# Late constants behind the fifth unit, decay and delta-rule products spread between units, three units chunk by chunk

## The chip, the cores and the metric

The kernel runs on one core of a Trainium2 chip. The metric is the device time of one execution in microseconds (us), as the median of several executions. TensorE (PE) multiplies, VectorE (DVE) and ScalarE (ACT) do the elementwise work, SyncE (SP) issues nearly all DMAs, and GpSimd (POOL) does nothing that matters here.

## The reference, cut to what matters

Two transformer blocks run on 256 tokens of width 1024. The first has three mixing branches (softmax attention with a decay, `ya`; a gated delta rule, `yb`; stick-breaking attention, `yc`), each gated and projected, then attention over 256 memory tokens and a feed-forward part with a convolution. The second has a retention/convolution mixer and a mixture of 64 experts. What the change touches is the delta rule of the first block, over chunks of 64 tokens:

```python
def step(state, xs):
    q_n, u_n, w_n, g_n, attn_n, kt_n, gl_n = xs
    v_new = u_n - jnp.einsum("bhck,bhkv->bhcv", w_n, state)
    o = (jnp.einsum("bhck,bhkv->bhcv", q_n * jnp.exp(g_n)[..., None], state)
         + jnp.einsum("bhce,bhev->bhcv", attn_n, v_new))
    state = state * jnp.exp(gl_n)[..., None, None] + jnp.einsum("bhck,bhcv->bhkv", kt_n, v_new)
    return state, o
```

There are four chunks and four heads. `decay` in the reference is the matrix exp(gc_i - gc_j) within a chunk, from the running sum `gc` of the gate's logarithm.

## The kernel before

**Units.** The dense weights come as 101 units of 1 MB (128 partitions x 2048 numbers), in the order of the list `UNITS`. SP loads each into one of `RAW` = 5 places of a ring. ACT rounds it to a high part (`ahead`, L1001, `w_high`, 3 places) and DVE takes the difference as the low part (`lows`, L1555, `w_low`, in the unit's own place). PE multiplies in three products for each 128x128 block: high by high, low by high, high by low (`product`, L323 to L325). A unit is 48 such matmuls with 256 columns. `unit` runs all eight input chunks for the first half of the outputs, then for the second; with `by_chunk=True` it runs both halves for a chunk before it goes to the next, so that it asks for a late chunk later. Before a chunk whose input may not be ready it waits (`chunk_ready`). `unit_tok` is the same with tokens as output rows, `unit_o` the one for four-chunk inputs.

**Order.** Each engine's order is written out by hand. In the program of SP (end of the listing), the first five units, x, and the constants are issued with no wait, and unit n waits for the end of unit n-5. `c1` holds constants; its first 744 columns are needed early, the other 4096 (2 MB), `rows_w` (272 KB) and `router_b` (36 KB) are the late ones. They stand ahead of unit 3 (`gk1`).

**Beginning.** PE multiplies `gq0`, the mean square of x, `gq1`, then `gk0`, which needs the normalised input: DVE scales chunks (L1522, `a_h`), ACT rounds them (L984, `h_high`), DVE takes the low part (L1519, `h_low`). On ACT the high part of unit 3 stands ahead of these roundings (`ahead(UNITS[0], 3)`, then `high_parts`). DVE then takes low parts of units and does the convolution taps of each unit (L1600).

**Decay.** After the units `fk0`, `fk1`, PE makes small products with four input rows: L433 (the per-token columns) and L440 (`decay0`, `decay1`: four matmuls of 256 columns that spread a row over all partitions). ACT takes their exponentials (L1087), DVE subtracts (L1658), and then `fv0`, `fv1` follow on PE.

**Delta rule.** `state_v(n)` (L564) multiplies the state; DVE makes `vnew(n)` of it; `state_o(n)` makes the output of chunk n: for each head one matmul with the state (L576, all 128 rows of the array, 64 columns) and one with `vnew` (L578, 64 rows, 64 columns), and then in the same function the state's increment (L586, `dS`, 64 rows, 128 columns), which DVE's `state(n)` adds (L1784, L1786). These steps, and the scores (`sb_scores`, L503) and sums (`sb_sums`, L513) of stick-breaking attention, stand between the units of the branches in the lists that `branch` is given.
**End.** After the dense units the experts run one after another; each expert's weights are 6 MB, and SP loads them as places come free.

## Time and profile before

| | |
|---|---|
| median of 3 runs | 1659.66 us (1658.47 to 1661.39) |
| span of the profiled execution | 1659.8 us |
| PE busy | 1357.1 us, 82% of the span |
| DVE busy | 643.6 us, 39% |
| ACT busy | 489.9 us, 30% |
| read from HBM | 515.81 MB, 311 GB/s over the span |

No separate time stands beside the profiled execution's span, and the span is within 0.2 us of the median. Times in the rows count from the span's start. PE's busy time counts a pipelined matmul as long as it takes from its start to its end, so that successive ones overlap: how long one really costs is the distance between starts. The granted clock (PEclk) is 1.00 at 2.4 GHz and 0.50 at 1.2 GHz.

### The profile page before, as it was taken

How to read it: one execution, taken by the hardware profiler on the slowest of the kernel's cores; microseconds unless marked ns; L12 is line 12 of the kernel's file. 1: busy time of each engine (PE TensorE's matmuls, PEld its weight loads, DVE VectorE, ACT ScalarE, POOL GpSimd, SP SyncE). 2: the span in 40 equal slices, each digit the busy share in tenths (PEclk: the TensorE clock that was granted, in tenths of full speed). 3: DMA queues.
4: the chain of work that ended last, by engine and by line, in shares of the span. 5: the costliest groups of instructions: out<-in, count | busy, mean ns of one | idle time of the engine just before them, and what ended most of it. 6: DMA issues, size and time to landing. Idle time of an engine off the chain costs nothing.

```text
span 1659.8 us, 32820 instructions
## 1 busy us (share of the span) xinstructions
PE 1357.1 (82%) x14402; PEld 1079.8 (65%) x14402; DVE 643.6 (39%) x1008; ACT 489.9 (30%) x819; POOL 0.2 (0%) x4
## 2 busy tenths in 40 slices
PE   8999999999999999998875766765585676567666
PEld 8998899999999999996543433433343343344333
DVE  6787735878787778663110100101110010111001
ACT  5766466456554455432000000000000000000001
POOL 0000000000000000000000000000000000000000
PEclk9999999999999999999998988988898898899889
DMA  7442023453446665488999999999999999999997
GB/s 300 160 146 102 27 102 104 176 195 136 177 180 243 229 246 193 150 350 362 428 425 432 426 429 434 429 428 428 430 429 430 431 429 425 432 430 429 428 431 321
DMA packets 41401, 517.93 MB, mean 312 GB/s; under 512 B 4720, under 2 KB 4848, under 8 KB 6384
## 3 DMA queue, kind: packets, MB, share of 16 engines
q1 hardware_dynamic: 41184, 516.71, 75.9%
q8 instruction: 55, 0.90, 0.2%
q10 hardware_dynamic: 144, 0.17, 0.0%
q14 instruction: 18, 0.15, 0.0%
HBM read 515.81 MB, written 1.05 MB: 311 GB/s over the span
## 4 chain that ended last, share of the span: by engine, by line
PE 47%; DMA 42%; DVE 6%; ACT 3%; issue 1%; SPq 1%; another core or an unknown queue 0%; DVEq 0%; ACTq 0%; PEldq 0%
DMA e_gu<-experts 41%; PE psum L323 10%; PE psum L324 9%; PE psum L325 9%; PE psum L887 6%; PE psum L928 3%; DVE w_low L1555 1%; DMA w_raw<-dense 1%; PE psum L541 1%; PE psum L383 1%; ACT w_high L1001 1%; PE psum L934 1%; PE psum L525 1%; PE psum L392 0%; PE psum L898 0%
## 5 line engine op out<-in xcount | busy, mean ns | idle before, releaser
L887 PE MATMUL psum<-e_gu,x_xt 128*32 128x256 f32 x3072 | 220.0, 450 | 172.7 <-DMA e_gu<-experts 172.7
L887 PEld LDWEIGHTS psum<-e_gu,x_xt 128*32 128x32 f32 x3072 | 109.4, 129 | 276.2 <-DMA e_gu<-experts 184.8
L323 PE MATMUL psum<-h_high,w_high 128*128 128x256 f32 x896 | 256.9, 287 | 4.6 <-DVE h_low L1519 3.6
L324 PE MATMUL psum<-h_low,w_high 128*128 128x256 f32 x896 | 253.7, 283 | 0.0
L325 PE MATMUL psum<-h_high,w_low 128*128 128x256 f32 x896 | 253.5, 283 | 0.0
L1555 DVE TENSOR_TENSOR w_low<-w_raw,w_high 128x2048 fp32r<-128x2048 f32 x100 | 228.5, 2288 | 38.0 <-ACT w_high L1001 33.0
L1001 ACT ACTIVATE w_high<-w_raw 128x2048 fp32r<-128x2048 f32 x100 | 191.2, 1914 | 71.4 <-PE psum L325 54.4
L2206 DVE COPY x_yb<-psum 128x256 f32<-128x256 f32 x64 | 27.2, 425 | 419.7 <-PE psum L928 419.7
L323 PEld LDWEIGHTS psum<-h_high,w_high 128*128 128x128 f32 x896 | 170.9, 191 | 6.1 <-issue 3.8
L324 PEld LDWEIGHTS psum<-h_low,w_high 128*128 128x128 f32 x896 | 171.2, 191 | 0.4 <-issue 0.2
L325 PEld LDWEIGHTS psum<-h_high,w_low 128*128 128x128 f32 x896 | 170.9, 191 | 0.0
L2204 DVE TENSOR_TENSOR x_act<-x_sil,psum 128x128 f32<-128x128 f32 x64 | 18.2, 285 | 335.7 <-ACT x_sil L1473 335.7
L928 PE MATMUL psum<-e_dn,x_actT 128*32 128x256 f32 x2048 | 126.7, 383 | 26.6 <-ACT x_actT L1477 25.3
L1473 ACT ACTIVATE x_sil<-psum 128x128 f32<-128x128 f32 x64 | 17.9, 279 | 431.6 <-PE psum L887 431.6
L928 PEld LDWEIGHTS psum<-e_dn,x_actT 128*32 128x32 f32 x2048 | 59.6, 109 | 75.2 <-issue 25.3
L1475 ACT ACTIVATE x_scat<-psum 128x256 f32<-128x256 f32 x64 | 24.6, 384 | 282.8 <-PE psum L914 280.8
L934 PE MATMUL psum<-x_yb,x_scat 32*128 32x256 f32 x1024 | 73.3, 400 | 34.8 <-DVE x_yb L2206 34.8
L934 PEld LDWEIGHTS psum<-x_yb,x_scat 32*128 32x128 f32 x1024 | 46.2, 184 | 67.1 <-DVE x_yb L2206 65.7
L898 PEld LDWEIGHTS psum<-x_s,x_htok 128*128 128x128 f32 x512 | 58.4, 192 | 5.7 <-issue 5.7
L898 PE MATMUL psum<-x_s,x_htok 128*128 128x128 f32 x512 | 61.4, 278 | 0.6 <-DVE x_s L2150 0.6
L1509 DVE RECIPROCAL all_sq<-all_sq 128x256 f32<-128x256 f32 (+1 forms) x25 | 50.1, 2004 | 12.8 <-ACTq L973 12.5
L323 PE MATMUL psum<-act_high,w_high 128*128 128x256 f32 x176 | 49.7, 282 | 1.2 <-DVE w_low L1555 1.1
(447 smaller groups left out, 2162.0 us busy)
## 6 DMA issues: line engine op xcount, KB each, us to landing
e_gu<-experts SPq DMA_DIRECT2D x44, 4096.0 KB, 52.9
w_raw<-dense SPq DMA_DIRECT2D x100, 1024.0 KB, 4.8
e_dn<-experts SPq DMA_DIRECT2D x46, 2048.0 KB, 49.4
e_dn<-experts SPq DMA_DIRECT2D x36, 1024.0 KB, 54.8
e_gu_lo<-experts SPq DMA_DIRECT2D x16, 2048.0 KB, 51.5
e_gu_hi<-experts SPq DMA_DIRECT2D x16, 2048.0 KB, 55.9
e_gu<-experts SPq DMA_DIRECT2D x8, 1024.0 KB, 8.1
e_gu<-experts SPq DMA_DIRECT2D x2, 2560.0 KB, 10.3
```

What stands on the lines that cost most here:

```text
L323: mm(ps, w[0], src[0], start=start, stop=False, **kw)
L324: mm(ps, w[0], src[1], start=False, stop=False, **kw)
L325: return mm(ps, w[1], src[0], start=False, stop=stop, **kw)
L887: last = mm(half(psum[32 * s:32 * s + 32, GU_BANK[j % 2], 0:256], P), X["xt"][:, k, CAP * j:CAP * (j + 1)], expert_gu(j, k)[:, :, s * P:(s ...
L898: last = mm(psum[:, 4 + c // 4, (c % 4) * P:(c % 4 + 1) * P], X["htok"][:, t, c * P:(c + 1) * P], X["s"][:, t, :], start=(t == 0), stop=(t ...
L928: last = mm(psum[32 * s:32 * s + 32, 7, 0:256], X["actT"][:, CAP * c:CAP * (c + 1)], expert_dn[j][:, c, s * T:(s + 1) * T], start=(c == 0) ...
L934: last = mm(psum[:, s, t * T:(t + 1) * T], X["scat"][32 * s:32 * s + 32, t * P:(t + 1) * P], X["yb"][32 * s:32 * s + 32, :], start=False, ...
L1001: ac(high(w), raw[:, place(w), :], ACT.Copy).then_inc(sem("w_high"), 1)
L1475: ac(X["scat"], psum[:, 7, 256:512], ACT.Copy).then_inc(sem("scatter_kept"), 1)
L1509: link(V.reciprocal(rs, rs))
L1555: V.tensor_tensor(low(w), raw[:, place(w), :], high(w).bitcast(F32), ALU.subtract).then_inc(sem("w_low"), 1)
L2206: V.tensor_copy(X["yb"], psum[:, 7, 0:256]).then_inc(sem("e_y"), 1)
```

## The change

Four edits. The three late constants are issued behind the first five units and before the wait for unit 0. `decay0` stands between the two halves of `fv0` and `decay1` behind `fv0`. In the delta rule, `state_o` makes the four products with the state first and then the four with `vnew`, in one accumulation group; the increment is a function of its own, `state_d`, called one unit later; DVE's `state(0)` and `state(1)` are moved down accordingly, and `state_v(3)` one unit down. `gk0`, `out00` and `q20` are run with `by_chunk=True`.

```diff
-            unit("gk0", HI, split_input("mix")); unit("gk1")
+            unit("gk0", HI, split_input("mix"), by_chunk=True); unit("gk1")
...
-            for q in range(2):
+            def decay(q):
...
-            unit_tok("fv0"); unit_tok("fv1")
+            unit_tok("fv0", between=lambda: decay(0)); decay(1); unit_tok("fv1")
...
+                for hd in range(H if n else 0):
+                    mm(ps[:, hd * CHUNK:(hd + 1) * CHUNK], A["state"][:, hd, :],
+                       A["gdn_qk"][:, hd, 0, n * CHUNK:(n + 1) * CHUNK], start=(hd == 0), stop=False,
+                       skip_group_check=True)
                 for hd in range(H):
                     un = t * H + hd
                     vn = A["vnew"][po:po + CHUNK, hd * P:(hd + 1) * P]
-                    if n:
-                        mm(ps[:, hd * CHUNK:(hd + 1) * CHUNK], A["state"][:, hd, :],
-                           A["gdn_qk"][:, hd, 0, n * CHUNK:(n + 1) * CHUNK], start=True, stop=False)
                     last = mm(ps[:, hd * CHUNK:(hd + 1) * CHUNK], vn,
-                              A["kd"][po:po + CHUNK, un, 0, po:po + CHUNK], start=(n == 0), stop=True)
+                              A["kd"][po:po + CHUNK, un, 0, po:po + CHUNK], start=(n == 0 and hd == 0),
+                              stop=(hd == H - 1), skip_group_check=True)
                 aux.filled(last, f"o{n}")
-                if n == T // CHUNK - 1:
-                    return
+
+            def state_d(n):
...
             branch("a", ya, "ya", [
-                lambda: (state_o(0), sb_scores(0)), lambda: sb_scores(1), lambda: state_v(1), lambda: sb_sums(0),
-                lambda: (sb_sums(1), state_o(1)), lambda: pv("spv", 0, "sb_a", A["pt"], A["sb_v"]),
+                lambda: (state_o(0), sb_scores(0)), lambda: (state_d(0), sb_scores(1)), lambda: state_v(1),
+                lambda: sb_sums(0), lambda: (sb_sums(1), state_o(1)),
+                lambda: (state_d(1), pv("spv", 0, "sb_a", A["pt"], A["sb_v"])),
...
             branch("c", yc, "yc", [
-                lambda: (sb_sums(2), sb_sums(3), state_v(3)),
-                lambda: (pv("spv", 2, "sb_a", A["pt"], A["sb_v"]), pv("spv", 3, "sb_a", A["pt"], A["sb_v"]), state_o(3)),
+                lambda: (state_d(2), sb_sums(2), sb_sums(3)),
+                lambda: (state_v(3), pv("spv", 2, "sb_a", A["pt"], A["sb_v"]), pv("spv", 3, "sb_a", A["pt"], A["sb_v"]), state_o(3)),
...
-            unit("out00", mixed, ("mixed", lambda k: k // 2 + 1)); unit("out01", mixed)
+            unit("out00", mixed, ("mixed", lambda k: k // 2 + 1), by_chunk=True); unit("out01", mixed)
...
-            unit("q20", r_gained, gained_input("n1"))
+            unit("q20", r_gained, gained_input("n1"), by_chunk=True)
...
-            state(0); lows("ga10"); sb_keep(0); lows("ga11"); sb_keep(1); mix("a", 0, 0); vnew(1); mix("a", 0, 1); sb_masked(0)
-            state(1); sb_masked(1); lows("oa_1"); sbout(0); mix("a", 1, 0); lows("gc00"); sbout(1); vnew(2); mix("a", 1, 1)
+            lows("ga10"); sb_keep(0); state(0); lows("ga11"); sb_keep(1); mix("a", 0, 0); vnew(1); mix("a", 0, 1); sb_masked(0)
+            sb_masked(1); lows("oa_1"); state(1); sbout(0); mix("a", 1, 0); lows("gc00"); sbout(1); vnew(2); mix("a", 1, 1)
...
             for n, name in enumerate(UNITS):
+                if n == RAW:
+                    sp.dma_start(A["rows_w"], rows_w_in).then_inc(sem("late_consts_loaded"), 16)
+                    sp.dma_start(c1[:, C1_EARLY:], c1_in[:, C1_EARLY:]).then_inc(sem("late_consts_loaded"), 16)
+                    sp.dma_start(rb, rb_in).then_inc(sem("late_consts_loaded"), 16)
                 if n >= RAW:
                     sp.wait_ge(*done[UNITS[n - RAW]])
...
-                if n == 3:
-                    sp.dma_start(A["rows_w"], rows_w_in).then_inc(sem("late_consts_loaded"), 16)
-                    sp.dma_start(c1[:, C1_EARLY:], c1_in[:, C1_EARLY:]).then_inc(sem("late_consts_loaded"), 16)
-                    sp.dma_start(rb, rb_in).then_inc(sem("late_consts_loaded"), 16)
```

**The order on SP**, its first DMAs. `w_raw` is a unit, `all_c` the constants. Before:

```order
L2295 DMA w_raw<-dense 128x2048
L2275 DMA all_c_58<-c 128x744
L2295 DMA w_raw<-dense 128x2048
L2277 DMA a_rows_w<-rows_w 128x544
L2278 DMA all_c_58<-c 128x4096
L2279 DMA all_rb<-router_b 128x72
```

With the change:

```order
L2302 DMA w_raw<-dense 128x2048
L2286 DMA all_c_58<-c 128x744
L2302 DMA w_raw<-dense 128x2048 x3
L2278 DMA a_rows_w<-rows_w 128x544
L2279 DMA all_c_58<-c 128x4096
L2280 DMA all_rb<-router_b 128x72
```

Units 3 and 4 have moved ahead of the late constants.

**The order on PE** around `state_o(1)`, between the units `ga10` and `ga11`. L576 multiplies the state, L578 (L582 with the change) `vnew`, L586 is the increment. Before:

```order
L515 MATMUL psum<-a_s,all_c_58 128x128
L576 MATMUL psum<-a_gdn_qk,a_state 128x64
L578 MATMUL psum<-a_kd,a_vnew 128x64
L576 MATMUL psum<-a_gdn_qk,a_state 128x64
L578 MATMUL psum<-a_kd,a_vnew 128x64
...
L586 MATMUL psum<-a_vnew,a_k_tail 128x128 x4
L323 MATMUL psum<-h_high,w_high 128x256
```

With the change:

```order
L518 MATMUL psum<-a_s,all_c_58 128x128
L576 MATMUL psum<-a_gdn_qk,a_state 128x64 x4
L582 MATMUL psum<-a_kd,a_vnew 128x64 x4
L323 MATMUL psum<-h_high,w_high 128x256
```

The two kinds of product no longer alternate, and the increment is gone from here: it stands behind the unit that follows.

**The order on DVE** in the same stretch, where the state is updated (L1786 before, L1793 with the change) and the low part of a unit is made (L1555, L1562). Before:

```order
L1811 TENSOR_TENSOR a_s<-psum,all_c_58 128x384
L1786 SCALAR_TENSOR_TENSOR a_state<-a_state,a_eg,psum 128x128 x4
L1811 TENSOR_TENSOR a_s<-psum,all_c_58 128x384
L1555 TENSOR_TENSOR w_low<-w_raw,w_high 128x2048
L1531 CAST yc_high<-psum 128x256
```

With the change:

```order
L1818 TENSOR_TENSOR a_s<-psum,all_c_58 128x384 x2
L1562 TENSOR_TENSOR w_low<-w_raw,w_high 128x2048
L1793 SCALAR_TENSOR_TENSOR a_state<-a_state,a_eg,psum 128x128 x4
L1538 CAST yc_high<-psum 128x256
```

The update has moved behind the low part of `oa_1`.

## Rows read from the trace of the kernel before

**Rows 1.** The page, part 2: granted clock and DMA share in 40 slices.

```profile
PEclk9999999999999999999998988988898898899889
DMA  7442023453446665488999999999999999999997
```

**Rows 2.** The page, part 4: the chain that ended last, shares by engine.

```profile
PE 47%; DMA 42%; DVE 6%; ACT 3%; issue 1%; SPq 1%; another core or an unknown queue 0%; DVEq 0%; ACTq 0%; PEldq 0%
```

**Rows 3.** Stretches: us, busy (x) of PE, PEld, DVE, ACT, POOL; PEclk, DMA, GB/s.

```profile
24.80:28.20 3.40, 0.17 (x2) 0.02 (x1) 0.83 (x2) 2.95 (x3) 0.00 (x0) 1.00 1.02 424
29.30:32.60 3.30, 3.09 (x14) 3.05 (x15) 2.96 (x8) 0.97 (x3) 0.00 (x0) 0.50 0.29 119
98.80:104.30 5.50, 5.50 (x26) 5.47 (x26) 5.00 (x9) 2.92 (x5) 0.00 (x0) 0.50 0.14 55
240.90:244.20 3.30, 3.30 (x17) 3.30 (x17) 2.81 (x6) 3.16 (x5) 0.00 (x0) 0.50 0.00 0
760.00:1640.00 880.00, 606.29 (x8389) 354.91 (x8388) 85.67 (x250) 63.51 (x205) 0.00 (x0) 0.90 1.00 428
```

**Rows 4.** Timeline of PE where it waited: start, us, instruction, idle before and releaser.

```profile
9.87 0.39 PE L323 MATMUL psum<-m_gained_high,w_high 128*128 128x256 f32 x1 [1.94 <-DVE w_low L1567]
28.21 0.36 PE L323 MATMUL psum<-h_high,w_high 128*128 128x256 f32 x1 [3.25 <-DVE h_low L1519]
48.57 0.38 PE L323 MATMUL psum<-h_high,w_high 128*128 128x256 f32 x1 [1.01 <-DVE w_low L1555]
132.36 0.48 PE L464 MATMUL psum<-a_gdn_qk 128*128 128x256 f32 x1 [0.94 <-ACT a_k_tail L1131]
345.81 0.38 PE L323 MATMUL psum<-mixed_high,w_high 128*128 128x256 f32 x1 [0.55 <-DVE mixed_low L1532]
628.22 0.39 PE L323 MATMUL psum<-r_gained_high,w_high 128*128 128x256 f32 x1 [0.70 <-DVE r_gained_low L1538]
```

**Rows 5.** Timeline of ACT at the beginning.

```profile
16.61 1.91 ACT L1001 ACTIVATE w_high<-w_raw 128x2048 fp32r<-128x2048 f32 x1 [1.31 <-DMA w_raw<-dense]
24.91 1.91 ACT L1001 ACTIVATE w_high<-w_raw 128x2048 fp32r<-128x2048 f32 x1 [5.04 <-DMA w_raw<-dense]
```

**Rows 6.** Timeline of DVE at the beginning.

```profile
22.55 1.67 DVE L1522 SCALAR_TENSOR_TENSOR a_h<-all_x,all_sm,all_sq 128x256 f32<-128x256 f32 x4
27.37 0.69 DVE L1519 TENSOR_TENSOR h_low<-a_h,h_high 128x512 fp32r<-128x512 f32 x1 [3.16 <-ACT h_high L984]
32.55 2.29 DVE L1555 TENSOR_TENSOR w_low<-w_raw,w_high 128x2048 fp32r<-128x2048 f32 x1 [0.24 <-DVE a_fox_q L1589]
46.22 2.29 DVE L1555 TENSOR_TENSOR w_low<-w_raw,w_high 128x2048 fp32r<-128x2048 f32 x1
```

**Rows 7.** Timeline of PE and ACT around and after the decay products.

```profile
96.30 2.60 PE L440 MATMUL psum<-a_rows,all_c 4*128 4x256 f32 x8
101.50 1.07 ACT L1087 ACTIVATE a_eg<-psum 128x512 f32<-128x512 f32 x2
116.53 1.92 ACT L1001 ACTIVATE w_high<-w_raw 128x2048 fp32r<-128x2048 f32 x1 [0.27 <-ACT all_sq L971]
120.66 0.47 ACT L971 ACTIVATE all_sq<-psum,all_c 128x256 f32<-128x256 f32 x1 [2.22 <-PE psum L392]
```

**Rows 8.** Timeline of PE in `state_o(0)` and `state_o(1)`, and of DVE after the latter.

```profile
213.58 1.10 PE L578 MATMUL psum<-a_kd,a_vnew 64*128 64x64 f32 x8
214.52 1.11 PE L586 MATMUL psum<-a_vnew,a_k_tail 64*128 64x128 f32 x8
236.95 0.33 PE L576 MATMUL psum<-a_gdn_qk,a_state 128*128 128x64 f32 x2
237.21 0.43 PE L578 MATMUL psum<-a_kd,a_vnew 64*128 64x64 f32 x2
239.66 1.11 PE L586 MATMUL psum<-a_vnew,a_k_tail 64*128 64x128 f32 x8
240.81 1.12 DVE L1786 SCALAR_TENSOR_TENSOR a_state<-a_state,a_eg,psum 128x128 f32<-128x128 f32 x4 [6.20 <-PE psum L586]
```

More of the change, by code:

```diff
@@ L352, in unit, with unit_tok @@
                 done[name] = proj.full(name)
-            def unit_tok(name, src=HI):
+            def unit_tok(name, src=HI, between=None):
                 w = parts(name, DC)
@@ L361, in unit_tok @@
                                        k == 0, k == DC - 1)
+                    if t == 0 and between:
+                        between()
                 proj.filled(last, name)
@@ L574, in state_o @@
                     vn = A["vnew"][po:po + CHUNK, hd * P:(hd + 1) * P]
-                    if n:
-                        mm(ps[:, hd * CHUNK:(hd + 1) * CHUNK], A["state"][:, hd, :],
-                           A["gdn_qk"][:, hd, 0, n * CHUNK:(n + 1) * CHUNK], start=True, stop=False)
                     last = mm(ps[:, hd * CHUNK:(hd + 1) * CHUNK], vn,
-                              A["kd"][po:po + CHUNK, un, 0, po:po + CHUNK], start=(n == 0), stop=True)
+                              A["kd"][po:po + CHUNK, un, 0, po:po + CHUNK], start=(n == 0 and hd == 0),
+                              stop=(hd == H - 1), skip_group_check=True)
                 aux.filled(last, f"o{n}")
-                if n == T // CHUNK - 1:
-                    return
+            def state_d(n):
+                t, po = n // 2, CHUNK * (n % 2)
                 ps = aux.fill(pe, f"dS{n}")
```

## The prediction

> **What bounds the kernel now.** I read the page's slices first [rows 1]: DMA is the bound in the second half, from about 760 us, and not before. There the engines move 428 GB/s at a share of 1.00 [rows 3], and the chain of waits puts 42% on DMA and 47% on PE [rows 2]. What the last 900 us cost is bytes over that rate, and the change doesn't touch it. Their start is set by the dense part, since SP issues the experts' weights as dense units finish. So time saved on PE ahead of 760 us should come off the end one for one. Then I looked in the dense part for stretches in which PE stood idle [rows 4] or ran at the lower clock [rows 3]. PE has no other slack there: each unit is 48 matmuls about 0.12 us apart.
>
> What PE did ahead of each fall of the clock is to be seen. At 28.21 it had been idle for 3.25 us [rows 4], and the granted clock was 0.50 for the next 3.3 us. It was 0.50 again after the tiny and four-row products that end at 98.8, for 5.5 us, and after `state_o(1)` with its increment, for 3.3 us [rows 3]; that last pattern stands three times, at 240.9, 261.4 and 281.9. PE was busy by the count in those stretches, but with matmuls that fill few columns or rows. Idle times of 1.94 and 1.01 us [rows 4] were not followed by a fall.
>
> **Late constants and `gk0`.** ACT's high part of unit 3 waited 5.04 us for its load and began at 24.91; that of unit 2 began at its landing, 16.61 [rows 5]. In these 8.3 us the queue moved 272 + 2048 + 36 KB of constants and 1024 KB of the unit, 3.46 MB, which is 417 GB/s, near the 424 of the stretch [rows 3]: the landings follow the order of issue. With the constants behind, unit 3 lands 2.5 us after unit 2, at about 19.1, and its high part is done by 21.8. The roundings then wait for DVE alone. DVE ends its four scalings at 22.55 + 1.67 = 24.2 and can take the first low part then rather than at 27.37 [rows 6]: 3.15 us earlier. The constants land at about 27.4 in place of 22.5; PE first asks for them behind `gv1`, at 54, so this costs nothing, and were that cover gone it would cost 5 us. Unit 5 waits for PE in both orders and finds the same bytes ahead of it.
>
> What does PE get of these 3.15 us? It starts `gk0` at 25.05, and by chunk it needs a pair of chunks every 1.4 us, about the pace at which DVE makes them (1.6 us): without `by_chunk` the first half would want all eight in 2.8 us. It is done at about 30.8. From there DVE is late: low part of unit 3 at 32.55 + 2.2 - 3.15 = 31.7, and that of unit 5 at 46.22 + 2.2 - 3.15 = 45.3 [rows 6], in a DVE program with hardly a gap between. PE would reach unit 5 at 43.3 and stand for 2.1 us, where it stood for 1.01 before. So all of DVE's 3.15 us arrive behind unit 5 and no more; the half-clock stretch at 29.3 costs nothing now, as DVE is behind anyway, and removing it gives nothing more. **Term: -3.15.** The new idle time of 2.1 us is between 1.94 without a fall and 3.25 with one, and nearest to the first, so I count no fall; with one, half of 3.3 us is lost and the term is -1.5. That is the other end.
>
> **Decay spread out.** The half-clock stretch of 5.5 us and the end of L440 [rows 3, 7] seem to offer up to 5.5/2 + 0.6 = 3.4 us on PE. But who waits for that? ACT's program holds both `eg` exponentials [rows 7] ahead of a high part, eight exponentials, two copies, eight squares, another high part, four roots and a third high part. From the end of the second exponential (102.57) to the end of that work (118.45) ACT is never idle for over 0.3 us. In the new order `decay1` stands behind two halves of `fv0`: 96.30 + 2.9 + 0.9 + 2.9 + 0.9 = 103.9 (24 matmuls at 0.12; four passes of L440 at about 0.22). Its exponential ends at 104.6, and the same 15.9 us of ACT work end at 120.5. Before, ACT waited for PE 2.22 us and began the next roots at 120.66. Behind them ACT already sets the pace: PE waits for `k_tail` at 132.36 [rows 4]. So ACT gains 0.2 us, and the rest of PE's gain becomes waiting of PE at the head sums and transposes around 120. **Term: -0.2**, with ends +1 (ACT slips by one more wait) and -3.4.
>
> **Delta rule.** `state_o(1)` takes 239.66 - 236.95 = 2.71 us for 16 passes, 0.17 us each; the eight passes of L578 alone in `state_o(0)` take 214.52 - 213.58 = 0.94, 0.12 each [rows 8]. Grouped, 16 passes cost about 1.9 us: 0.8 saved, three times, 2.4; the ends are 0 and 2.4. The increment costs the same 1.04 wherever it is. Cutting the run of 3.8 us of such products to 1.9, with the increment behind a full unit, leaves less quiet work than `state_o(0)` with its increment (0.94 + 1.04 = 1.98), which was not followed by a fall. So three falls vanish, each half of at least 3.3 us: about 1.6 each, 4.8; the ends are 0 and 5.
>
> Who waits for the moved steps? DVE's `state(1)` waited 6.20 us for PE [rows 8] and is moved behind a low part of 2.2 us; the increment comes at 245.7 now, when DVE is free, and `state_v(2)` follows at about 250. `state(0)` has two us to spare in the same way. The bank of `o1` now waits for the release by `sb_masked(0)`, done at 234.6, 2.3 us ahead. Only `state_v(3)` is now close to its user: `vnew(3)`, then the low part of `oc_0` on DVE take 0.1 + 0.9 + 2.2 us, about as long as the products PE has in between; I charge 0.1. **Term: -(2.4 + 4.8 - 0.1) = -7.1.**
>
> By the Trainium skill, page "TensorE: Matmul & The Clock Gate", section "The mechanism", a weight load overlaps running matmuls only when its row group differs; by that rule the grouped order loses overlap and gains nothing, and the sum would be 2.4 us smaller. The trace speaks against it, as L578 alone costs 0.12 and the mix 0.17; it is a rival below.
>
> **`out00` and `q20`.** PE idles for 0.55 us at 345.81 for the last chunks of `mixed` and for 0.70 us at 628.22 for chunks of the second block's input [rows 4]. By chunk they are wanted 2.1 and 0.4 us later (each earlier chunk takes 0.71 instead of 0.36 us). DVE's next low parts have room. **Term: -1.25**; ends -0.8 and -1.6.
>
> **Sum.** 3.15 + 0.2 + 7.1 + 1.25 = 11.7 us. The profiled span was 1659.8, the median 1659.66, so both bases agree: 1659.66 - 11.7 = 1648.0 us.
>
> **Rivals.**
> 1. *The clock falls stay*, because 1.9 us of narrow products next to scores or sums is still quiet enough, and it falls ahead of unit 5 too. For it: the runs of `sb_sums` and `pv` stand next to `state_o`. Against it: `state_o(0)`. Loss of 4.8 + 1.6 us: 1654.4.
> 2. *Grouping gives nothing*: it is the passes with the state that are slow, not the alternation (no row shows L576 alone). 2.4 us less: 1650.4.
> 3. *The decay gain arrives after all*, as ACT's work turns out to start earlier than I chained it: 3 us more: 1645.0.
> 4. *Unit 3 does not land earlier*, if the queue shares among transfers in flight: no 3.15: 1651.2. The landing at 16.61, before 2 MB issued behind it, speaks against it.
> 5. *Slower: DVE becomes the bound of the delta rule.* `state(1)` behind `lows("oa_1")` depends on ACT's high part, and `state_v` and `state_o` on PE depend on DVE. If DVE came over 3 us late at each of the three steps, PE would idle 3.25 us and the clock would fall for another 1.6, three times 4.85 = 14.5: 1648.0 + 14.5 = 1662.5. Of the 6.20 us that DVE waited there [rows 8], 2.2 go to the low part that now stands ahead, so it decides from the point where DVE or the high part it needs is 4 us later than before at each step; no single operation on DVE or ACT in the stretch is that long.
>
> **How the numbers follow.** Forecast 0.58, rival 1 0.13, rival 2 0.09, rival 3 0.08, rival 4 0.08, rival 5 0.04. The range takes in rivals 2, 3 and 4 and single falls that stay: 1644.5 to 1652.5; beyond it lie rivals 1 and 5, 17 in 100. 0.2% is 3.3 us, about what a measurement of this kernel can tell. All cases but rival 5 are faster by more; for mixtures of several small losses I leave 0.03 to the same: 0.93, 0.03, 0.04.
>
> **What would show it.** Right: high part of unit 3 begins near 19.9 with no wait for its load; `gk0` near 25.0; PE idle about 2 us ahead of unit 5; L576 at 0.12 us a pass; PEclk 1.00 from the first unit to 630; small waits of PE near 117 to 124, and the wait for `k_tail` still there; the experts' start 11 to 12 us earlier. Wrong: a half-clock stretch behind a `state_o`, a new wait of over 1 us for `vnew` or `state`, or a dense part that ends earlier while the experts' part grows.

## The result and the profile after

The changed kernel takes 1651.01 us (median of 4 runs, 1649.94 to 1651.4), the one before 1659.07 us (4 runs, 1657.8 to 1661.39). The ratio is 0.995 with a 95% interval of 0.9939 to 0.9962: 6 to 10 us faster. It is faster as forecast and inside the range, 3.0 us above the forecast of 1648.0. Two runs of the later comparisons were several times as long, 7237.73 us for the kernel before and 5277.15 us for `out00` and `q20` alone, and are left out of every range, number of runs and ratio.

The profiled execution of the changed kernel has a span of 1649.0 us and took 1650.75 us: the time is the span and 1.8 us. That holds in every profile below.

The page of the changed kernel, parts 2 and 4: granted clock in 40 slices, and the shares of the chain that ended last.

```profile
PEclk9999999999999999999998988988898899899889
...
PE 45%; DMA 42%; DVE 8%; ACT 3%; issue 1%; SPq 1%; another core or an unknown queue 0%; DVEq 0%; ACTq 0%; PEldq 0%
```

Ahead of the experts, in the first 18 slices, the clock reads just as in [rows 1]: the slices round a fall of 3.4 us away. The stretches show what changed. They are those of [rows 3], moved with the work: us, busy (x) of PE, PEld, DVE, ACT, POOL; PEclk, DMA, GB/s.

```profile
24.80:28.20 3.40, 3.40 (x30) 3.39 (x29) 3.30 (x8) 1.43 (x3) 0.00 (x0) 1.00 1.00 406
29.30:32.60 3.30, 2.53 (x22) 2.33 (x21) 3.18 (x4) 2.72 (x3) 0.00 (x0) 1.00 0.57 156
96.20:101.40 5.20, 5.20 (x34) 4.24 (x33) 4.70 (x10) 0.70 (x2) 0.00 (x0) 1.00 0.09 30
236.90:240.20 3.30, 3.30 (x31) 3.30 (x30) 0.13 (x1) 3.17 (x5) 0.00 (x0) 1.00 0.07 30
760.00:1640.00 880.00, 600.50 (x8351) 351.13 (x8352) 82.88 (x236) 64.55 (x207) 0.00 (x0) 0.91 1.00 427
```

All stretches that stood at 0.50 before are at 1.00. PE, idle but for 0.17 us from 24.8 to 28.2 before, works through it. And the second half is as it was: share 1.00, 427 GB/s.

The timeline of PE in the changed kernel at its waits and at the first product of the experts' part (last line), as in [rows 4]: start, us, instruction, idle before and releaser.

```profile
9.54 0.39 PE L323 MATMUL psum<-m_gained_high,w_high 128*128 128x256 f32 x1 [1.28 <-DVE w_low L1574]
25.06 0.35 PE L323 MATMUL psum<-h_high,w_high 128*128 128x256 f32 x1
31.74 0.39 PE L323 MATMUL psum<-h_high,w_high 128*128 128x256 f32 x1 [0.77 <-DVE w_low L1562]
45.40 0.39 PE L323 MATMUL psum<-h_high,w_high 128*128 128x256 f32 x1 [1.83 <-DVE w_low L1562]
117.65 0.41 PE L457 MATMUL psum<-all_c,a_gdn_qk 128*128 128x128 f32 x2 [0.93 <-ACTq L239]
128.59 0.48 PE L467 MATMUL psum<-a_gdn_qk 128*128 128x256 f32 x1 [0.91 <-ACT a_k_tail L1138]
748.25 0.79 PE L905 MATMUL psum<-x_s,x_htok 128*128 128x128 f32 x5 [0.56 <-DVE x_s L2157]
```

`gk0` starts at 25.06 instead of 28.21. Unit 5 comes 3.17 us earlier, behind 1.83 us of idle time in place of 1.01. The waits for `mixed` and for the second block's input (345.81 and 628.22 before) have no successor. The same first product of the experts in the profile before:

```profile
759.79 0.68 PE L898 MATMUL psum<-x_s,x_htok 128*128 128x128 f32 x4 [0.56 <-DVE x_s L2150]
```

So the experts' part starts 11.54 us earlier. From there to the end it is 900.0 us before and 900.7 after; over all profiles of this study it lies between 899.7 and 900.7. What PE saves ahead of the experts comes off the end.

ACT at the beginning and at the decay, in the changed kernel, as in [rows 5, 7]:

```profile
16.69 1.92 ACT L1008 ACTIVATE w_high<-w_raw 128x2048 fp32r<-128x2048 f32 x1 [1.14 <-DMA w_raw<-dense]
20.36 1.92 ACT L1008 ACTIVATE w_high<-w_raw 128x2048 fp32r<-128x2048 f32 x1 [0.25 <-ACT all_sq L978]
98.36 0.58 ACT L1094 ACTIVATE a_eg<-psum 128x512 f32<-128x512 f32 x1
101.48 0.60 ACT L1094 ACTIVATE a_eg<-psum 128x512 f32<-128x512 f32 x1 [2.54 <-PE psum L443]
```

Unit 3's high part no longer waits for its load. The second exponential of the decay waits 2.54 us for its products, which are now behind half a unit.

PE in `state_o(1)` with its increment a unit later, and DVE's update behind it, in the changed kernel, as in [rows 8]:

```profile
233.74 1.00 PE L576 MATMUL psum<-a_gdn_qk,a_state 128*128 128x64 f32 x8
234.67 1.10 PE L582 MATMUL psum<-a_kd,a_vnew 64*128 64x64 f32 x8
241.57 1.16 PE L592 MATMUL psum<-a_vnew,a_k_tail 64*128 64x128 f32 x8
242.76 1.12 DVE L1793 SCALAR_TENSOR_TENSOR a_state<-a_state,a_eg,psum 128x128 f32<-128x128 f32 x4 [5.73 <-PE psum L592]
```

Eight passes with the state take 234.67 - 233.74 = 0.93 us, and those with `vnew` 1.03 (the unit behind starts at 235.70): 1.96 where 2.71 stood.

### The profile page after: what moved, and what is told of

The parts are those of the page before. It is cut to its first block, busy times and chain, and to the rows that moved or that the text cites. A ratio compares the mean times of both kernels' runs of the same rounds, so it can differ in the third digit from the quotient of the medians.

```text
span 1649.0 us, 32820 instructions
## 1 busy us (share of the span) xinstructions
PE 1345.0 (82%) x14402; PEld 1069.4 (65%) x14402; DVE 643.2 (39%) x1008; ACT 489.4 (30%) x819; POOL 0.2 (0%) x4
## 4 chain that ended last, share of the span: by engine, by line
PE 45%; DMA 42%; DVE 8%; ACT 3%; issue 1%; SPq 1%; another core or an unknown queue 0%; DVEq 0%; ACTq 0%; PEldq 0%
DMA e_gu<-experts 41%; PE psum L323 9%; PE psum L324 9%; PE psum L325 9%; PE psum L894 7%; PE psum L935 3%; DVE w_low L1562 2%; DVE all_sq L1516 1%; PE psum L385 1%; PE psum L544 1%; ACT w_high L1008 1%; DMA w_raw<-dense 1%; PE psum L941 1%; PE psum L905 0%; DVE a_gdn_qk L1607 0%
## 5 line engine op out<-in xcount | busy, mean ns | idle before, releaser
L1562 DVE TENSOR_TENSOR w_low<-w_raw,w_high 128x2048 fp32r<-128x2048 f32 x100 | 228.4, 2288 | 46.5 <-ACT w_high L1008 41.6
```

The costliest lines, as they stand in the source:

```text
L1562: V.tensor_tensor(low(w), raw[:, place(w), :], high(w).bitcast(F32), ALU.subtract).then_inc(sem("w_low"), 1)
```

## The experiments

One thing has to be known to read them: **the clock falls are not the same in every execution.** So each profile is read at two marks: PE's wait for `k_tail` (132.36 before, [rows 4]) and the start of the experts' part. The stretch up to the first mark is called the first part, the one between the marks the second part. "Fall at 98" means a stretch at the granted clock 0.50 that starts there, of 3.4 us if nothing else is said.

### The kernel before, once more

> The kernel before, unchanged, profiled anew. Theory A (the profile on which the sum was made was one execution with many falls of PE's clock; another execution has other falls): the span differs from 1659.8 us by 1 to 4 us, the falls stand at other places or are fewer than the five in the first profile, each missing fall takes about 1.6 us off the start of the experts' part (759.8 us in the first profile), and the time from there to the end stays at 900 us within 1. Theory B (the falls are the same in every execution, and the experts' part of the changed kernel gives 3 us back): the same five falls at the same instructions, experts' start at 759.8 within 0.5, span 1659.8 within 1.

Nothing is edited. Measured: 1658.95 us (12 runs, 1657.49 to 1661.86) beside 1658.41 of the same kernel (23 runs, 1656.0 to 1661.54), ratio 1.0003 (0.9994 to 1.0011). The profile has other falls than the first: at 11 and at 28, and one of 6.8 us at 257. There is none at the decay and none at 240.9.

Stretches in this profile, columns as above:

```profile
28.30:31.60 3.30, 3.28 (x14) 3.26 (x15) 3.20 (x7) 1.26 (x2) 0.00 (x0) 0.50 0.71 283
98.00:104.00 6.00, 6.00 (x50) 5.67 (x48) 5.50 (x7) 2.48 (x4) 0.00 (x0) 1.00 0.31 126
240.90:244.20 3.30, 3.30 (x30) 3.30 (x30) 2.28 (x1) 1.91 (x3) 0.00 (x0) 1.00 0.00 0
257.10:263.70 6.60, 6.60 (x32) 6.38 (x32) 3.11 (x8) 6.04 (x8) 0.00 (x0) 0.50 0.00 0
```

The same program did the same work around 98 and 240.9, this time at 1.00. Its two marks:

```profile
130.14 2.16 PE L464 MATMUL psum<-a_gdn_qk 128*128 128x256 f32 x8 [0.94 <-ACT a_k_tail L1131]
756.21 0.68 PE L898 MATMUL psum<-x_s,x_htok 128*128 128x128 f32 x4 [0.56 <-DVE x_s L2150]
```

The experts start 3.58 us earlier than in the first profile: 2.22 us in the first part, 1.36 in the second. So the profile on which the prediction rests had lost more to the clock than others do. Over 94 runs of this kernel in the whole study the times go from 1655.6 to 1661.9 us, mean 1658.8; the first profile's, 1659.8 + 1.8 = 1661.6, is among the highest.

### The changed kernel, once more

> The changed kernel, unchanged, profiled anew. Theory A: the experts' part starts at 748.2 us plus 1.6 for each fall of the clock that this execution has and the first did not (0 or 1 of them, likeliest in the idle time of 1.8 us ahead of unit 5); time about 8 us below before. Theory B: start at 748.2 within 0.5, and from there to the end about 901 to 904 us.

Measured: 1650.9 us (5 runs, 1649.63 to 1651.79), ratio 0.995 (0.9938 to 0.9963). The marks are 128.48 and 748.19, and there is no fall of the clock from the first unit to the experts. The marks of the two profiles of the changed kernel agree to 0.1 us, and its 5 runs lie within 2.2 us, where 12 runs of the kernel before took up 4.4.

### The delta rule's part alone

```diff
+                for hd in range(H if n else 0):
+                    mm(ps[:, hd * CHUNK:(hd + 1) * CHUNK], A["state"][:, hd, :],
...
-                if n == T // CHUNK - 1:
-                    return
+            def state_d(n):
...
-                lambda: (state_o(0), sb_scores(0)), lambda: sb_scores(1), lambda: state_v(1), lambda: sb_sums(0),
+                lambda: (state_o(0), sb_scores(0)), lambda: (state_d(0), sb_scores(1)), lambda: state_v(1),
```

> The kernel before with the delta rule's edits alone (products grouped, increment a unit later, DVE's updates moved). Of the 11.5 us by which the experts start earlier in the profile, the prediction puts 7.1 here: experts' start about 752.7 in an execution that has the other falls. Theory A: the time is 3.5 to 5 us below before, since the falls behind state_o do not come in every execution, 2.2 us of it from the grouping, which is there in all. Theory B: 7 us below before, less what the experts' part gives back.

Measured: 1653.48 us (5 runs, 1653.04 to 1653.8), ratio 0.9965 (0.9952 to 0.9978). Marks 130.08 and 751.57; the only fall is at 28.6, ahead of DVE's late low part of unit 3. This is the largest part of the change: 5.8 us by the ratio (3.6 to 8.0). The five runs lie within 0.8 us, but five are too few to say that the spread goes with the falls at `state_o`.

### The beginning alone

```diff
-            unit("gk0", HI, split_input("mix")); unit("gk1")
+            unit("gk0", HI, split_input("mix"), by_chunk=True); unit("gk1")
...
+                if n == RAW:
+                    sp.dma_start(A["rows_w"], rows_w_in).then_inc(sem("late_consts_loaded"), 16)
...
-                if n == 3:
-                    sp.dma_start(A["rows_w"], rows_w_in).then_inc(sem("late_consts_loaded"), 16)
```

> The kernel before with the late constants behind the fifth unit and gk0 by chunk, nothing else. By the prediction DVE's 3.15 us arrive behind unit 5 (PE starts it at 45.4 in place of 48.6) and PE idles 1.8 to 2.1 us ahead of it: 3.1 us below before, 1.5 where the clock falls in that idle time. Theory B says the same of the start and nothing of the end.

Measured: 1657.35 us (11 runs, 1654.78 to 1659.14), ratio 0.9991 (0.9982 to 1.0). Unit 5 and the stretch behind it:

```profile
45.25 0.39 PE L323 MATMUL psum<-h_high,w_high 128*128 128x256 f32 x1 [1.83 <-DVE w_low L1555]
```

```profile
46.20:49.50 3.30, 3.30 (x18) 3.30 (x17) 3.12 (x5) 0.00 (x0) 0.00 (x0) 0.50 0.43 176
```

Unit 5 starts 3.3 us earlier, but here the clock fell behind the 1.83 us of idle time. In the changed kernel the same 1.83 us stand at the same place, and no fall follows. So the other end of the front's term, a fall at unit 5, is a thing that happens, in some executions. Here it took about 1.4 of the 3.15 us: the first mark is 128.99, with a further fall at 97.3, and the table below puts that one at 0.6. By the ratio the beginning gives 1.5 us (0 to 3.0), less than the 3.15 of an execution without a fall there.

### The decay alone

```diff
-            for q in range(2):
+            def decay(q):
...
-            unit_tok("fv0"); unit_tok("fv1")
+            unit_tok("fv0", between=lambda: decay(0)); decay(1); unit_tok("fv1")
```

> The kernel before with the decay products spread, nothing else. Theory C (ACT's order sets the pace: the exponential of decay1 stands ahead of 15.9 us of ACT work, so it is a loss of about 1.7 us against an execution of the kernel before without a fall at the decay, and a gain of 0.2 to 0.6 against one with 6.8 us of half clock there): the wait for k_tail ends at about 131.7 us in every execution (before: 130.1 and 132.4), PE waits for ACT near 120.5, median within 1 us of before. Theory D (the spread products save PE's half-clock time and the end gets it): 2 to 3.4 us below before.

Measured: 1659.58 us (12 runs, 1657.86 to 1661.61) beside 1659.53, ratio 1.0001 (0.9992 to 1.0009): level. Its profile has no fall at the decay. The waits of PE behind it are these:

```profile
120.71 0.30 PE L457 MATMUL psum<-all_c,a_gdn_qk 128*128 128x128 f32 x1 [0.93 <-ACTq L239]
131.65 0.48 PE L467 MATMUL psum<-a_gdn_qk 128*128 128x256 f32 x1 [0.92 <-ACT a_k_tail L1134]
```

The first mark is 131.65: 1.5 us **later** than in the second profile of the kernel before, which had no fall there either (130.14), and 0.7 earlier than in the first, which had one of 6.8 us. So the edit gives back a fall where there is one and costs 1.5 to 1.6 us where there is none. Falls there are common: of the ten profiles in this study with the decay products together, six have one of 3.4 or 6.8 us at the decay; of the four with them spread, none.

ACT in that second profile of the kernel before says why:

```profile
101.64 1.07 ACT L1087 ACTIVATE a_eg<-psum 128x512 f32<-128x512 f32 x2
102.59 1.92 ACT L1001 ACTIVATE w_high<-w_raw 128x2048 fp32r<-128x2048 f32 x1
...
116.65 1.91 ACT L1001 ACTIVATE w_high<-w_raw 128x2048 fp32r<-128x2048 f32 x1 [0.27 <-ACT all_sq L971]
118.47 0.46 ACT L971 ACTIVATE all_sq<-psum,all_c 128x256 f32<-128x256 f32 x1
```

Without the fall, ACT takes the roots (L971) at 118.47 with no wait. The wait of 2.22 us for PE ahead of them in [rows 7] was itself the fall's doing. ACT in the decay alone, the high part behind the second exponential and the same roots:

```profile
105.04 1.91 ACT L1004 ACTIVATE w_high<-w_raw 128x2048 fp32r<-128x2048 f32 x1
...
120.06 0.46 ACT L974 ACTIVATE all_sq<-psum,all_c 128x256 f32<-128x256 f32 x1
```

With the decay spread, that high part starts 2.45 us later (105.04 and 102.59) and the roots 1.6 us later (120.06 and 118.47). So ACT's work between takes up 0.9 us of the delay, and the rest reaches the roots.

### All but the decay

The changed kernel with L443's two steps ahead of `fv0` again:

```diff
-            def decay(q):
+            for q in range(2):
...
-            unit_tok("fv0", between=lambda: decay(0)); decay(1); unit_tok("fv1")
+            unit_tok("fv0"); unit_tok("fv1")
```

> The changed kernel with the decay products as before. Theory C: where the clock does not fall at them, the wait for k_tail ends at 126.9 rather than 128.6 us and the experts start at 746.5 rather than 748.2; where it falls for 6.8 us, 749; the median is 0 to 1.5 us below the changed kernel, or level if falls are frequent. Theory D: slower than the changed kernel by 2 to 3.4 us.

Measured: 1649.02 us (6 runs, 1648.21 to 1650.48), ratio 0.9937 (0.9924 to 0.9949). A fall at 95.3 is there in the profile, and still the first mark is 127.58, 1.0 us earlier than in the changed kernel. The interval overlaps that of the changed kernel (0.9939 to 0.9962), so that taking the decay edit out makes the kernel faster is seen in the mark and not settled by the times.

### The decay spread, and ACT's order with it

If ACT is what the decay's term turns on, a high part placed in ACT's wait should take the loss away. In the changed kernel, on ACT, the high part of `fk1` moves between the two exponentials:

```diff
+                if q == 0:
+                    ahead("fk1")
-            ahead("fk1")
```

> The changed kernel with one line moved on ACT: the high part behind the decay exponentials is made between the two of them, in the 2.5 us in which ACT waits for PE's second decay product. Theory C: all of ACT's later work is 1.7 us earlier, the wait for k_tail ends near 127.0, the experts start at 746.6, time 1.6 us below the changed kernel. Theory D: no change, as ACT was not what PE waited for.

Measured: 1648.89 us (6 runs, 1648.04 to 1650.07), ratio 0.9936 (0.9923 to 0.9948). The timeline of ACT:

```profile
98.15 0.58 ACT L1094 ACTIVATE a_eg<-psum 128x512 f32<-128x512 f32 x1
98.63 1.91 ACT L1008 ACTIVATE w_high<-w_raw 128x2048 fp32r<-128x2048 f32 x1
101.28 0.60 ACT L1094 ACTIVATE a_eg<-psum 128x512 f32<-128x512 f32 x1 [0.74 <-PE psum L443]
```

and of PE at the two marks:

```profile
126.75 2.16 PE L467 MATMUL psum<-a_gdn_qk 128*128 128x256 f32 x8 [0.93 <-ACT a_k_tail L1139]
746.28 0.79 PE L905 MATMUL psum<-x_s,x_htok 128*128 128x128 f32 x5 [0.56 <-DVE x_s L2158]
```

The wait of 2.54 us is 0.74, the first mark is 1.84 us earlier than in the changed kernel, and no fall is left anywhere ahead of the experts. Its median is the lowest of the study: 10.6 us below that of the kernel before in the same comparison, and 2.1 us below the changed kernel's. That last difference stands across comparisons; by the ratios' intervals, 0.9923 to 0.9948 and 0.9939 to 0.9962, it isn't settled, but the marks show where it comes from. It is level with all but the decay, 1649.02 us: spreading the decay with ACT's order mended gives no more in the times than leaving the decay as it was.

### `out00` and `q20` alone

```diff
-            unit("out00", mixed, ("mixed", lambda k: k // 2 + 1)); unit("out01", mixed)
+            unit("out00", mixed, ("mixed", lambda k: k // 2 + 1), by_chunk=True); unit("out01", mixed)
...
-            unit("q20", r_gained, gained_input("n1"))
+            unit("q20", r_gained, gained_input("n1"), by_chunk=True)
```

> The kernel before with out00 and q20 by chunk alone. The two idle times (0.55 at 345.8, 0.70 at 628.2) go, no new one comes: 1.2 us below before; from the end of ob_1 to the end of q21 1.25 us less in any execution, whatever its falls.

Measured: 1657.73 us (11 runs, 1655.63 to 1658.28) beside 1659.53, ratio 0.9987 (0.9978 to 0.9996). The profile has the three falls of the first profile of the kernel before in its second part, and that part is 756.14 - 130.75 = 625.39 us against 759.79 - 132.36 = 627.43: 2.0 us less, where 1.25 were forecast. The two waits show 0.55 + 0.70 us of idle time; from the unit at 320.14 to the one at 460.72 in the first profile, in which `out00` lies, the second profile of the kernel before takes 140.6 us and this one 139.8; from there to the experts, with `q20`, it is 299.1 and 297.9. So 0.8 and 1.2 us went, more than the idle time. PE's rows at the two waits, in the second profile of the kernel before, show why:

```profile
341.38 0.28 PE L325 MATMUL psum<-mixed_high,w_low 128*128 128x256 f32 x1
342.21 0.39 PE L323 MATMUL psum<-mixed_high,w_high 128*128 128x256 f32 x1 [0.56 <-DVE mixed_low L1532]
342.43 0.28 PE L324 MATMUL psum<-mixed_low,w_high 128*128 128x256 f32 x1
...
623.66 0.28 PE L325 MATMUL psum<-r_gained_high,w_low 128*128 128x256 f32 x1
624.64 0.39 PE L323 MATMUL psum<-r_gained_high,w_high 128*128 128x256 f32 x1 [0.70 <-DVE r_gained_low L1538]
624.87 0.28 PE L324 MATMUL psum<-r_gained_low,w_high 128*128 128x256 f32 x1
```

Inside a unit the starts are 0.12 us apart. Here they are 0.83 apart and then 0.22, which is 0.81 us more; in `q20` they are 0.98 and then 0.23, which is 0.97 more, and five shorter delays of 0.04 to 0.05 us around the wait bring it to 1.2. The idle time is counted only from the end of the matmul ahead, 0.28 us after its start, and so understates the loss.

### The grouping alone, and the moved increment alone

```diff
+                for hd in range(H if n else 0):
+                    mm(ps[:, hd * CHUNK:(hd + 1) * CHUNK], A["state"][:, hd, :],
+                       A["gdn_qk"][:, hd, 0, n * CHUNK:(n + 1) * CHUNK], start=(hd == 0), stop=False,
...
-                    if n:
-                        mm(ps[:, hd * CHUNK:(hd + 1) * CHUNK], A["state"][:, hd, :],
-                           A["gdn_qk"][:, hd, 0, n * CHUNK:(n + 1) * CHUNK], start=True, stop=False)
```

> The kernel before with the products of state_o grouped (four with the state, then four with vnew), the increment still right behind. From the profile of the changed kernel the grouping saves 2.71 - 1.96 = 0.75 us at each of three places, 2.25 in every execution. If it is the length of the run of narrow products that lets the clock fall, the run is cut from 3.8 to 3.0 us and falls should be fewer but still come: median 2.3 to 5 us below before, spread of the runs over 1.5 us. If the grouping alone takes the falls away, the runs lie as close together as those of the delta edits together (1653.0 to 1653.8) at about 1653.5.

Measured: 1652.93 us (11 runs, 1652.28 to 1654.7) beside 1658.08 (33 runs), ratio 0.9971 (0.9962 to 0.998). The increment stands right behind `state_o` here, and still there is no fall in the second part, in this stretch as in any other (in the first part there are two, of 6.8 us at 27 and of 3.4 at 98.6):

```profile
240.00:243.40 3.40, 3.40 (x31) 3.40 (x30) 2.53 (x2) 3.13 (x4) 0.00 (x0) 1.00 0.00 0
```

By the ratio it gives 4.8 us (3.3 to 6.3). The passes themselves give 2.5 of it, so the falls that no longer come are worth some 2.3 us on average, an estimate. The 11 runs lie within 2.4 us. The expectation took a spread of over 1.5 us as a sign that falls still come, so the spread speaks for neither side; it has falls of the first part in it. PE in its `state_o(1)`, then the increment and the unit behind it:

```profile
235.29 1.00 PE L573 MATMUL psum<-a_gdn_qk,a_state 128*128 128x64 f32 x8
236.22 1.10 PE L579 MATMUL psum<-a_kd,a_vnew 64*128 64x64 f32 x8
237.16 1.11 PE L588 MATMUL psum<-a_vnew,a_k_tail 64*128 64x128 f32 x8
238.20 0.39 PE L323 MATMUL psum<-h_high,w_high 128*128 128x256 f32 x1
```

The other half of the edit, with the products still alternating:

```diff
-                if n == T // CHUNK - 1:
-                    return
+            def state_d(n):
...
-            state(0); lows("ga10"); sb_keep(0); lows("ga11"); sb_keep(1); mix("a", 0, 0); vnew(1); mix("a", 0, 1); sb_masked(0)
+            lows("ga10"); sb_keep(0); state(0); lows("ga11"); sb_keep(1); mix("a", 0, 0); vnew(1); mix("a", 0, 1); sb_masked(0)
```

> The kernel before with the increment a unit later (and the DVE and state_v moves), the products of state_o alternating as before. If the length of the run decides, it is cut from 3.8 to 2.7 us: falls fewer or gone, median 1 to 3.5 us below before. If the alternation itself decides (0.18 us for 64 columns), the falls stay and the median is that of before.

Measured: 1657.49 us (11 runs, 1656.38 to 1660.0), ratio 0.9999 (0.999 to 1.0008): nothing. A fall at 257 remains, so moving the increment doesn't reliably keep the clock up. That it makes falls a little rarer isn't excluded, since the move costs 0.7 us of its own (below) and the time is level:

```profile
257.30:260.50 3.20, 3.20 (x16) 3.20 (x17) 1.12 (x2) 3.14 (x6) 0.00 (x0) 0.50 0.01 3
```

The move even costs a little. From the unit ahead of `state_o(0)` to the end of the first unit of `yc`, the grouping alone takes 280.23 - 206.05 = 74.18 us, and the grouping with the move (the third experiment) 280.38 - 205.48 = 74.90: 0.72 more. PE's rows in the latter at `state_o(1)`:

```profile
235.97 1.10 PE L579 MATMUL psum<-a_kd,a_vnew 64*128 64x64 f32 x8
237.00 0.39 PE L323 MATMUL psum<-h_high,w_high 128*128 128x256 f32 x1
```

Eight `vnew` passes take 1.03 us when a product on the whole array follows, and 0.94 (236.22 to 237.16 above) when the increment follows, which is on 64 rows too. Each place where the form of the array changes costs about 0.1 us: 0.09 here. Ungrouped, a `state_o` has six such changes more and takes 2.71 - (0.93 + 0.94) = 0.84 us longer, 0.14 each; the moved increment makes two more at each of three places, for 0.72 us, 0.12 each.

### The late constants alone, and `gk0` alone

The first of these has only the DMAs moved, the second only this line:

```diff
-            unit("gk0", HI, split_input("mix")); unit("gk1")
+            unit("gk0", HI, split_input("mix"), by_chunk=True); unit("gk1")
```

> The kernel before with the late constants behind the fifth unit and gk0 in its old order. DVE's first low part of the input at 24.2 us all the same, but PE wants all eight chunks in the first 2.8 us of gk0 and waits inside it; since DVE is what arrives last at unit 5 (45.3), the gain there is the same 3.1 us, and by_chunk has no part in it: median 2 to 3 us below before.

> The kernel before with gk0 by chunk alone, constants in their old place. PE starts gk0 at 28.2 as before and DVE's chain is unmoved, so unit 5 starts at 48.6 and nothing is gained: level with before within 0.5 us, unless the clock's fall at 28 us lasts long enough to make PE the later one.

Measured: late constants 1655.94 us (11 runs, 1654.5 to 1659.02), ratio 0.9989 (0.998 to 0.9998); `gk0` by chunk 1659.65 us (11 runs, 1657.52 to 1661.89), ratio 1.0008 (0.9999 to 1.0017), beside the same 1658.08. So the constants give 1.8 us (0.3 to 3.3) by the ratio, and `gk0` by chunk nothing that stands clear of its interval. Unit 5, with the late constants moved:

```profile
45.30 0.39 PE L323 MATMUL psum<-h_high,w_high 128*128 128x256 f32 x1 [1.69 <-DVE w_low L1555]
```

and with `gk0` by chunk alone:

```profile
48.51 0.39 PE L323 MATMUL psum<-h_high,w_high 128*128 128x256 f32 x1 [1.55 <-DVE w_low L1555]
```

The constants bring unit 5 forward to 45.30, and with `gk0` by chunk as well it is at 45.25. So the whole front gain is the constants'; `by_chunk` on `gk0` gives nothing, alone or on top, because DVE's low parts of units 3 and 5 set the pace behind it either way.

### All profiles in one sum

The sum below compares profiles, each of one execution. The first part of the kernel before without a fall that counts is 130.1 us (two profiles, 130.14 and 130.08). Its second part without one is that of the grouping alone and the three times 0.84 us that the grouping saves: 620.72 + 2.5 = 623.2. Falls at 10 to 30 us don't show in the first part and are not counted. What the edits and other falls add is taken from one pair of profiles each:

| | first part | second part | from |
|---|---|---|---|
| late constants | -3.15 | | unit 5 in the changed kernel |
| decay spread | +1.6 | | decay alone, 131.65 |
| fall of 3.4 / 6.8 us at the decay | +0.6 / +2.3 | | 130.75 (`out00` and `q20` alone) / first profile |
| grouping | | -2.5 | passes, 3 x 0.84 |
| moved increment | | +0.7 | 74.90 - 74.18 |
| each 3.4 us of fall near `state_o` | | +1.4 | first profile, (627.43 - 623.2)/3 |
| `out00` and `q20` | | -2.0 | these alone |

The sum then gives the other profiles:

| kernel | first part: sum, measured | second part: sum, measured |
|---|---|---|
| before, again (6.8 us at 257) | (130.1), 130.14 | 626.0, 626.07 |
| beginning alone (at 46 and at the decay, three) | (129.0), 128.99 | 627.4, 627.36 |
| delta rule alone (no fall) | (130.1), 130.08 | 621.4, 621.49 |
| decay alone (6.8 us at 239) | (131.7), 131.65 | 626.0, 626.06 |
| all but decay (one at the decay) | 127.6, 127.58 | 619.4, 619.37 |
| ACT's order too (none) | 127.0, 126.75 | 619.4, 619.53 |
| moved increment alone (one) | 130.1, 129.95 | 625.3, 625.48 |
| late constants alone (6.8 us at the decay, three) | 129.3, 129.19 | 627.4, 627.45 |
| `gk0` alone (two) | 130.1, 129.79 | 626.0, 626.12 |
| changed kernel (none) | 128.6, 128.59 | 619.4, 619.66 |

Values in brackets are those the sum was made from. The rest agree within 0.3 us. The kernel before with no fall would take 130.1 + 623.2 + 900.2 + 1.8 = 1655.3 us, with 900.2 for the experts' part as the middle of its 899.7 to 900.7; its lowest run of 94 took 1655.6. So falls cost its average execution 1658.8 - 1655.3 = 3.5 us, and the one that was profiled first 759.79 - 753.3 = 6.5 us.

## Why the prediction was right, and where it was off

**The bound and the place.** Right. DMA's second half kept its 880 us at a share of 1.00, and 11.54 us saved ahead of it came off the span but for the 0.7 us by which the experts' part differed.

**Late constants and `gk0`, -3.15.** Right in every step, which the changed kernel's own profile shows: high part of unit 3 at 20.36 with no wait for the load (19.9 forecast), `gk0` at 25.06 (25.05), unit 5 at 45.40 (45.3) behind 1.83 us of idle time (2.1). The other end, a fall there, was shown by the front alone. That `by_chunk` on `gk0` had a part in it was not right. In the times the edit gives less than the term, 1.8 us (0.3 to 3.3) for the constants alone and 1.5 (0 to 3.0) with `gk0`; a fall at unit 5 in some executions would account for that. Nor does the length of the idle time tell when that happens, as the prediction took it to: 1.94 us at 9.87 had no fall behind it in the first profile, 2.06 and 2.02 at the same place had none in the delta rule alone and `gk0` alone, but 2.18 us had one in the second profile of the kernel before, and 1.83 at unit 5 had one in the beginning alone.

**Decay, -0.2.** Between the two profiles it gave 2.3 - 1.6 = 0.7 us. Against an execution with no fall there it costs 1.6. The fall was misread too: it began at 97.5, before L440's products ended, and lasted 6.8 us; the row of [rows 3] holds only its last 5.5. The step that failed is "Before, ACT waited for PE 2.22 us and began the next roots at 120.66": that wait was taken as slack of the program, and it was a by-product of the fall which the same edit was to take away. ACT's slip itself was near: its second exponential ends at 105.15 in the decay alone, 104.6 in the prediction. The end named for it, +1 by one more wait of ACT, was on the right side and too small.

**Delta rule, -7.1.** By profile pair it gave 2.5 - 0.7 + 4.2 = 6.0 us. Grouping was put at 2.4 and gave 2.5 in the passes; the three falls gave 4.2 us where 4.8 were forecast. But "the increment costs the same 1.04 wherever it is" was wrong by 0.7 us in all, in changes of the array's form. And the clock was kept up by the grouping alone, not by cutting the run of narrow products in two, as the argument on `state_o(0)` had it: with the increment right behind, nothing fell; with the increment moved and the products alternating, one fell. In the times, grouping alone gave 4.8 us (3.3 to 6.3), of which 2.3 for falls: half of the 4.8 forecast for them. The Trainium skill, page "TensorE: Matmul & The Clock Gate", section "The mechanism", lets a weight load overlap running matmuls only where its row group differs. The prediction drew from this that grouping loses overlap; but the passes with the state take all 128 rows and so the rows of those with `vnew` too, and by that rule alternating them has no overlap either. Here grouped passes with the state take 0.12 us (0.93 for eight), and the alternating ones 0.17. Nor does the trace agree with that rule: from 24.8 to 28.2 in the changed kernel every matmul takes all 128 rows, and the weight loads are busy for 3.39 of the 3.40 us, beside matmuls that are busy throughout. The page "TensorEngine Tiling (Array Packing)", section "Key Properties", says that a change of tiling mode drains the engine; the 0.1 us at each change agree with that, though no row shows a drain as such.

**`out00` and `q20`, -1.25.** The mechanism was right, the size not: 2.0 us. The step that failed is that only the idle time of the two rows was counted, 0.55 and 0.70 us; by the starts of the matmuls, these waits cost 0.8 and 1.2.

**The sum and its base.** By profile pair the terms are 3.15 + 0.7 + 1.8 + 4.2 + 2.0 = 11.9 us, against 11.7 forecast and 11.54 measured. That the sum comes so near is in part luck: the delta rule gave 1.1 us less than its term, the decay 0.5 and `out00` and `q20` 0.75 more. The forecast of the time was 3 us too low because of one sentence: "The profiled span was 1659.8, the median 1659.66, so both bases agree." They didn't: the time is the span and 1.8 us, which makes that execution one of 1661.6 us, about as slow as the slowest run that it was shown with (1661.39), by the falls that it happened to have. The terms for the falls, 4.8 us, were worked out from that execution and taken off a median that holds only about half as much of falls. With the fall-free difference, 1655.3 - 1650.3 (748.25 + 900.2 + 1.8) = 5.0 us, and the average loss to falls of 3.5 us, 8.5 us are accounted for; the medians are 8.06 apart.

**Rivals.** *The clock falls stay*: no, there are none in either profile of the changed kernel; its highest run, 1651.79, leaves room for one. *Grouping gives nothing*: no, 2.5 us. *The decay gain arrives after all*: no. Even with ACT's order changed, the time is that of leaving the decay alone (1648.89 and 1649.02 us). *Unit 3 does not land earlier*: no. *DVE becomes the bound*: no, its update still waits for PE, 5.73 us. That the result lies near the times of the second and fourth rivals is chance: neither's mechanism is there.

**What stays open.** The same idle time of 1.83 us was followed by a fall in the front alone and not in the changed kernel. The runs show that it varies, not what decides it. Nor is it shown why the clock falls behind alternating passes and not behind grouped ones; the runs show that it does. How often the changed kernel has a fall was seen in two profiles only, and neither ACT's order nor all but the decay was measured beside the changed kernel in one comparison.

## What to carry to other kernels

Before a saving from the clock is counted, profile the kernel twice: a fall that is there in one execution and not in the next is worth only its average, and a wait that it causes elsewhere is no slack. Set the profiled execution's time, not its span, beside the median before subtracting anything. Read what a wait costs from the distance between the starts of the matmuls, not from the idle time. On TensorE, keep products of one array form together, an increment right behind its kin included; when a step is spread to later places, look at what stands in line behind its reader, here ACT, and fill that wait from the work in the line, or leave the step where it was.

## What was not expected of the hardware

- The same program on the same data ran with five falls in one execution and three in the next, at other places: total 20.4 us at 0.50 ahead of the experts in the first (3.4 at 29.2, 6.8 at 97.5, three of 3.4 from 240.9), 13.6 in the second. Falls may also be what spreads the run times (6.3 us over 94 runs), but that isn't shown: of the kernels with 11 or 12 runs, the one with grouped products spreads over 2.4 us and those with alternating products over 2.7 to 4.5.
- Sixteen passes that alternate between 128 and 64 rows of the array, in which PE is busy by the count, were followed by falls in every profile that has them, though not at each of the three places; the same sixteen in two groups never were, in six profiles of five programs.
- A change of the array's form costs 0.09 to 0.14 us each time, at a clock of 1.00.
